# The memory layer's output product: weight chunk ahead of modulation chunk in the stream, and two groups of modulation sums inside the last weight chunk

## What is computed

```python
mod = cond @ ada_w[i] + ada_b[i]                       # modulation: 6 rows of 1024
sh_m, sc_m, g_m, sh_f, sc_f, g_f = split(mod, 6)
y = ((h * norm_w + skip * xc) * silu(z)) @ w_out       # w_out: 2048 x 1024, the output product
x = layer_norm(ALPHA * x + (1 + g_m) * y, ln_mix_g, ln_mix_b)
u = x * (1 + sc_f) + sh_f
y = swiglu(u, ffn_w13, ffn_w2)
```

## Time and profile before

| | |
|---|---|
| runs | 2980.57, 2975.04, 2979.97 us; median 2979.97 |
| the profiled execution | 2976.49 us, span 2974.4 us |
| PE matmul busy | 2817.2 us (95%) |
| VectorE busy | 1589.6 us (53%) |
| ScalarE busy | 599.5 us (20%) |
| DMA | 733.31 MB, 247 GB/s over the span |
| mean granted TensorE clock | 0.985 of full |

### The profile page before, as it was taken

How to read it: one execution, slowest core, us unless ns; L and a number is a source line. 1 busy time by engine, 2 the same in 40 slices (tenths; PEclk the granted TensorE clock), 3 DMA queues, 4 the chain that set the end, 5 groups by cost and what they waited for, 6 DMA issues and landing times.

```text
span 2974.4 us, 67823 instructions
## 1 busy us (share of the span) xinstructions
PE 2817.2 (95%) x28798; PEld 2508.9 (84%) x28798; DVE 1589.6 (53%) x3030; ACT 599.5 (20%) x1431; POOL 15.6 (1%) x27
## 2 busy tenths in 40 slices
PE   5999999999999999999999989999799999989887
PEld 4999898899999998889999867998678766867664
DVE  6776673267578567515666555889842111212113
ACT  1112113121121111321111220123521110111111
POOL 0000000000000000000000000000000000000000
PEclk8999999999999999999999999999899999999999
DMA  7665664346556557534565526782248889889995
GB/s 311 252 239 220 247 232 193 130 155 238 217 196 264 207 227 275 213 114 162 196 242 198 214 86 252 298 330 100 86 186 324 336 335 382 364 314 428 428 428 247
DMA packets 55553, 733.31 MB, mean 247 GB/s; under 512 B 6609, under 2 KB 6793, under 8 KB 10805
## 3 DMA queue, kind: packets, MB, share of 16 engines
q1 hardware_dynamic: 51364, 716.68, 60.6%
q0 software_dynamic: 3984, 13.74, 1.3%
HBM read 729.31 MB, written 4.23 MB: 247 GB/s over the span
## 4 chain that ended last, share of the span: by engine, by line
PE 82%; DMA 10%; DVE 5%; issue 2%; ACT 1%; SPq 0%; DVEq 0%; ACTq 0%
PE psum L761 36%; PE psum L852 18%; PE psum L1347 11%; PE psum L1398 5%; PE psum L839 3%; DMA work<-in_down_e_dram 3%; DMA work<-in_up_e_dram 2%; DMA ring<-in_up_dram 2%; PE psum L755 2%; PE psum L1414 1%; DMA ring<-in_w_v_dram 1%; DVE ring L1909 1%; DMA ring<-in_w_ccch_dram 1%; PE psum L1373 1%; DMA ring<-in_ada_dram 1%
## 5 line engine op out<-in xcount | busy, mean ns | idle before, releaser
L761 PE MATMUL psum<-work,ring 128*128 128x128 f32 x3680 | 440.8, 275 | 2.2 <-ACT work L1491 2.2
L761 PEld LDWEIGHTS psum<-work,ring 128*128 128x128 f32 x3680 | 425.2, 192 | 3.0 <-issue 1.6
L761 PE MATMUL psum<-work 128*128 128x128 f32 x3328 | 390.6, 276 | 3.2 <-DVE work L2003 1.9
L761 PEld LDWEIGHTS psum<-work 128*128 128x128 f32 x3328 | 381.6, 193 | 3.7 <-issue 3.2
L1909 DVE SCALAR_TENSOR_TENSOR ring<-ring,cond 128x1024 f32<-128x1024 f32 x240 | 279.3, 1220 | 84.9 <-DMA ring<-in_ada_dram 84.7
L852 PE MATMUL psum<-work,ring 128*128 128x256 f32 x1344 | 296.3, 383 | 6.3 <-DMA ring<-in_m_out_dram 4.1
L852 PEld LDWEIGHTS psum<-work,ring 128*128 128x128 f32 x1344 | 257.7, 192 | 43.5 <-DMA ring<-in_m_out_dram 4.9
L852 PE MATMUL psum<-h_t,ring 128*128 128x256 f32 x1280 | 278.9, 380 | 1.0 <-ACT h_t L1612 1.0
L852 PEld LDWEIGHTS psum<-h_t,ring 128*128 128x128 f32 x1280 | 242.6, 190 | 36.0 <-issue 3.1
L761 PE MATMUL psum<-h_t,ring 128*128 128x128 f32 x2272 | 266.6, 276 | 4.3 <-DMA ring<-in_up_dram 3.3
L761 PEld LDWEIGHTS psum<-h_t,ring 128*128 128x128 f32 x2272 | 260.0, 192 | 7.1 <-DMA ring<-in_up_dram 4.4
(11 more groups left out here) (402 smaller groups left out, 2807.3 us busy)
## 6 DMA issues: line engine op xcount, KB each, us to landing
ring<-in_ada_dram SPq DMA_DIRECT2D x60, 2048.0 KB, 8.1
ring<-in_up_dram SPq DMA_DIRECT2D x55, 2048.0 KB, 8.5
ring<-in_up_e_dram SPq DMA_DIRECT2D x32, 2048.0 KB, 9.2
work<-in_up_e_dram SPq DMA_DIRECT2D x32, 2048.0 KB, 9.8
ring<-in_down_dram SPq DMA_DIRECT2D x20, 2816.0 KB, 10.6
ring<-in_down_e_dram SPq DMA_DIRECT2D x16, 2048.0 KB, 10.0
work<-in_down_e_dram SPq DMA_DIRECT2D x16, 2048.0 KB, 11.6
ring<-in_w_qk_dram SPq DMA_DIRECT2D x12, 2048.0 KB, 8.5
```

Of the source, the lines that this page charges most:

```text
L761: mm = pe.matmul(bank(bank_of)[:, pair * P:(pair + 1) * P], w, right(i), start=(first and pair == 0 and i == 0), stop=(pair == lin.pairs - ...
```

## The change

```diff
-        "m_out": Linear(4, 2, 32 * P, "m_out", 4, order="amamamam"), "ln0": ln_fused,
+        "m_out": Linear(4, 2, 32 * P, "m_out", 4, order="mamamama"), "ln0": ln_fused,
```

```diff
                 if j == p.what.chunks - 1:
                     ada_sums(place("up3"))(0, 0, place("up3").slot(0))
+                    out_sums(p.what.adas - 1, 0, last_ada(p))
                 add_out(j, i, where)
 
-            walk(p, loop(p), out_chunk, ada_sums(p, 4 * DT))
+            out_sums = ada_sums(p, 4 * DT)
+            walk(p, loop(p), out_chunk, lambda n, i, where: out_sums(n, i, where) if n < p.what.adas - 1 else None)
```

## The result

| | before | with the change |
|---|---|---|
| median | 2979.69 us (14 runs) | 2983.99 us (14 runs) |
| lowest to highest | 2973.93 to 2982.73 | 2981.52 to 2987.35 |
| span of the profiled execution | 2974.4 us | 2979.8 us |

The ratio is 1.0021, with a 95% interval of 1.0013 to 1.0028: the change makes the kernel slower, by 6.3 us by the ratio (3.9 to 8.3), though the two medians lie only 4.3 us apart. The forecast was +6.5 us, 2985.0 us, in a range of 2978 to 2991.

A forecast was written before the change was run, and what follows sets the result against it. The prediction took TensorE to carry 82% of the chain, with VectorE and TensorE reaching the stage's end together. It summed +4.9 us for the last addition and +1.6 us for the clock to +6.5 us, 2985 us, range 2978 to 2991.

The forecast's parts named there:

- The gap ahead of m1 goes, and with it the low clock in m1.: Output product on TensorE: the 3.86 us gap and 1.8 us of low clock go, the stage 5.7 us shorter on TensorE alone.
- A0's load hangs on a2's sums and takes 8.8 us.: End of the output product: a2's sums release A0's buffer at 1833.3, and A0 lands at 1842.1.
- Nine microseconds of sums, the last addition 4.9 us later.: VectorE at the stage's end: eight sums, 9.2 us, where four stood; last addition 4.9 us later (3.8 to 6.0).
- The clock's price of 1.6 us.: TensorE in the mean: low clock after a new gap of about 10.9 us costs 1.6 us (nothing to 5.2).
- Nothing absorbs the shift.: From the norm through A1's sums to M2's load: nothing seen that would absorb a later norm.
- +6.5: Whole kernel: the sum of +4.9 us for the last addition and +1.6 us for the clock, 0.22%.
- M0, A1 and M1 later at no cost.: Loads behind A0: they go out later, the norm hides M0's; at most 3.5 us for M0 without that cover.
- the third rival: Stage's end: A0 and a3 summed when m3 ends, so TensorE sets the end, 5.7 us earlier, 2972; chance 0.04.
- The prediction's 1.9 us for the skill's order: Mean on TensorE: if the clock is already low at the restart, the price is 1.9 us and the sum +6.8.

The follow-up runs named there:

- e6: The changed kernel with a0's sums made early, in VectorE's wait ahead of the gates; 2985.44 us against 2977.84, ratio 1.0023.
- e1: The changed kernel with a3's sums made before A0's instead of after; 2980.86 us against 2978.17, ratio 1.0006.
- e4: The kernel before, old order string kept, with a0's sums made early in VectorE's wait ahead of the gates; 2972.04 us against 2978.17, ratio 0.9980.
- e7: e4 with a1's sums also moved, from behind to ahead of m0's additions; 2971.98 us against 2977.84, ratio 0.9976.
- e2: The kernel before with the new order string alone, a3's sums behind m3's additions; 2988.13 us against 2978.17, ratio 1.0034.

## Why the prediction was right, point by point

- *The gap ahead of m1 goes, and with it the low clock in m1.* Right: no wait in the four weight chunks. m3 ends 1840.7 - 1799.0 = 41.7 us after m0, forecast 42.0, before 47.7.
- *A0's load hangs on a2's sums and takes 8.8 us.* Right to a tenth: issued at about 1831.9, on VectorE at 1840.74, and the view of the loads gives 8.8 us to landing. Before, the same load took 7.7 us alone.
- *Nine microseconds of sums, the last addition 4.9 us later.* It is 4.6 us later, counted from m0's end. The step from m0's end to A0's issue was 0.3 us shorter than forecast (32.8 us, not 33.1; m2's load landed in 8.4 us, not 8.8, and did not hold TensorE up).
- *The clock's price of 1.6 us.* 1.2 us with the change, 1.5 and 1.7 in e6 and e1. The size was right within the bounds, the order of events was not, see below. The sum has a slip of its own: by its terms the fillers end and the 16 matmuls begin at 1857.3, which leaves them 0.6 us of low clock until 1857.9, not 0.9, and makes the price 1.4. In the trace the 16 lose nothing (3.62 us; 3.69 before); the price stands in the mean's matmuls (1.19 and 1.06 us; 0.60 and 0.67 before) and the fillers (2.22; 1.28 before).
- *Nothing absorbs the shift.* Right to M2's issue, where all 5.8 us are left, and the times of e4 and e6 confirm it for a gain and a loss. What follows M2's issue takes between 1099 and 1107 us in the nine profiled executions, with no relation to the edits that I can name; this scatter is as large as the effect, which is why single spans are not compared here.
- *How close +6.5 came is in part luck.* The trace has 5.8 us where the terms had 6.5, the ratio's interval is 3.9 to 8.3, and 2985.0 lies within 1.0 us of the measured median because the base taken, 2978.2, was 1.5 us under the later median of the kernel before.
- *M0, A1 and M1 later at no cost.* Right: in the changed kernel M0 starts on a wait for ScalarE's output, as before, and neither A1's sums nor M1 wait for a load. e1 leaves M0's load at m3's end and takes back 3.7 us all the same.
- *A remark under the third rival was misleading:* that putting a3 first would not help. It would not let TensorE set the end, but it takes away 4.2 us of the last addition's delay. The prediction had the means to see it: a3 landed four microseconds or more ahead of A0, in a wait of 8.9 us.
- The third rival, TensorE at the end, came true in e7, where the last addition waits 1.27 us for m3's last group; in e4 VectorE and TensorE end together. The rival wanted A0's buffer freed some 9 us earlier, with eight sums behind A0's landing. With the old string there are four, and 4.4 us earlier were enough in e4 (28.7 us after m0's end; the prediction followed it to 33.1).

## What to carry to other kernels

In a ring where each buffer is freed by one of two engines, ask of every moved chunk which engine now frees which load. Exchanging the neighbours all along a stage's stream changes the releaser of the load that closes the stage, and what stands behind that load. Here a load freed by the faster event, m2's end, came to hang on VectorE's sums behind it, eight sums followed it instead of four, and the time that TensorE gained stood as idle time ahead of the mean. Before moving work toward the end of a stage, look for a wait of the same engine further ahead: with the old string, four sums were worth 5.3 us when moved some 65 us earlier.

## What the runs showed of the hardware

The clock fell inside the gap, not after the restart as in the shorter gap of the earlier trace rows. Busy time by stretch of the changed kernel, from m3's end on (the seventh figure is the granted clock):

```profile
1840.70:1843.00 2.30, 0.00 (x0) 0.00 (x0) 2.26 (x3) 0.00 (x0) 0.00 (x0) 1.00 0.62 142
1843.00:1845.00 2.00, 0.00 (x0) 0.00 (x0) 2.00 (x5) 0.00 (x0) 0.00 (x0) 1.00 0.97 410
1845.00:1847.00 2.00, 0.00 (x0) 0.00 (x0) 2.00 (x5) 0.00 (x0) 0.00 (x0) 0.54 1.02 434
1847.00:1849.00 2.00, 0.00 (x0) 0.00 (x0) 2.00 (x5) 0.00 (x0) 0.00 (x0) 0.50 0.10 41
1849.00:1851.60 2.60, 0.00 (x0) 0.01 (x1) 2.36 (x6) 0.00 (x0) 0.00 (x0) 0.50 0.47 95
1851.60:1855.00 3.40, 3.38 (x12) 3.04 (x13) 2.45 (x13) 0.37 (x2) 2.55 (x5) 0.50 0.90 376
1855.00:1859.20 4.20, 4.20 (x23) 3.79 (x23) 1.97 (x7) 2.39 (x8) 0.61 (x2) 0.95 0.94 397
```

Full for the first 4.3 us of idling, 0.50 until the restart and on to about 1855.4 (0.95 over the last row's 4.2 us), then full. This is the order that the Trainium skill gives (TensorE: Matmul & The Clock Gate, section Part 1: The HAM clock gate), where the idle array is at half rate and activity releases it. The trace agrees in this gap, and in those of 10.10 us (e6), 6.04 us (e1) and 5.96 us (e2): 0.50 at the restart. It does not in the two short ones, 3.86 us and e2's 3.17 us, where the clock was 1.00 at the end of the gap and fell in the work behind it. The prediction's 1.9 us for the skill's order was still too much, although it left out the first two matmuls of the mean: the clock rose 3.8 us after the restart, not the 4.8 us that lie between 1853.1 and 1857.9.

A gap of 6.04 us (e1) cost no less than one of 10.96: 1.7 against 1.2 us. What goes with the price is how long the clock stays low behind the restart. Read in windows of 1 us, that is 3.8 us with the change, 4.5 in e6 and 4.9 in e1, for prices of 1.2, 1.5 and 1.7 us. These are three profiled executions, and what sets that length stays open.
